# A hybrid decoder block's down projection as a 2x2 block product with seven block products

## What is computed

```
D_MODEL = 1024
D_FF = ((8 * D_MODEL + 3 * 256 - 1) // (3 * 256)) * 256        # 2816

def swiglu(hn, w_gate, w_up, w_down):
    return (jax.nn.silu(hn @ w_gate) * (hn @ w_up)) @ w_down

h = h + swiglu(rms_norm(h, norm_ffn_g[l]), w_gate[l], w_up[l], w_down[l])
return rms_norm(h, norm_final_g)
```

## Time and profile before

| | |
|---|---|
| median of three runs | 3043.88 us |
| the profiled execution's own time | 3043.22 us |
| its span, first to last instruction | 3041.5 us |
| PE (matmuls) busy | 2956.7 us, 97% |
| DVE busy | 1627.4 us, 54% |
| POOL busy | 1255.0 us, 41% |
| ACT busy | 1069.0 us, 35% |
| DMA: moved, mean rate | 297.39 MB, 98 GB/s |
| matmuls of both down projections | 2112 |
| mean granted clock of TensorE | 0.996 |

### The profile page before, as it was taken

The page is one execution under the profiler, slowest core; times in us unless marked ns, Lnnn a source line. Parts: engine busy times, 40 slices in busy tenths (PEclk is TensorE's granted clock), DMA queues, the critical chain, the costliest instruction groups (busy, mean ns, idle before and its releaser), DMA issues. The chain is left out here.

```text
span 3041.5 us, 41966 instructions
## 1 busy us (share of the span) xinstructions
PE 2956.7 (97%) x14334; PEld 2449.6 (81%) x14334; DVE 1627.4 (54%) x2236; ACT 1069.0 (35%) x1975; POOL 1255.0 (41%) x1126
## 2 busy tenths in 40 slices
PE   7999999999999999999999999999999999999998
PEld 7888788878878888878888778887888788887887
DVE  2564566645366444445565456665635644444445
ACT  4522445424233333322233244542423333332212
POOL 6422454452224444454442244445221444445433
PEclk9999999999999999999999999999999999999999
DMA  6622222141112222253322232224111122225221
GB/s 231 213 94 103 91 83 70 59 169 42 61 65 77 83 83 83 83 193 112 124 98 87 103 102 72 69 66 163 56 56 70 56 83 83 83 83 193 83 111 76
DMA packets 131685, 297.39 MB, mean 98 GB/s; under 512 B 11825, under 2 KB 52849, under 8 KB 131569
## 3 DMA queue, kind: packets, MB, share of 16 engines
q1 hardware_dynamic: 69072, 226.07, 21.4%
q10 hardware_dynamic: 62496, 69.78, 6.7%
HBM read 222.37 MB, written 73.43 MB: 97 GB/s over the span
## 5 line engine op out<-in xcount | busy, mean ns | idle before, releaser
L2409 DVE TENSOR_TENSOR h<-h,PS 128x1024 f32<-128x1024 f32 x272 | 330.9, 1220 | 332.0 <-PE PS L2588 214.9
L2586 PE MATMUL PS<-act_hi,w_hi 128*128 128x512 f32 (+1 forms) x1088 | 428.5, 394 | 9.5 <-issue 5.5
L1535 DVE TENSOR_TENSOR copied<-copied,PS 128x512 f32<-128x512 f32 x308 | 207.5, 685 | 400.9 <-PE PS L2588 387.9
L2588 PE MATMUL PS<-act_hi,w_lo 128*128 128x512 f32 (+1 forms) x1088 | 406.6, 374 | 0.0
L2587 PE MATMUL PS<-act_lo,w_hi 128*128 128x512 f32 (+1 forms) x1088 | 405.6, 373 | 0.0
L2050 POOL TENSOR_TENSOR w_lo<-raw,w_hi 128x256 fp32r<-128x256 f32 (+1 forms) x144 | 193.8, 1369 | 435.0 <-ACT w_hi L2127 435.0
L611 POOL TENSOR_TENSOR part_lo<-sum_s,part_hi 128x512 fp32r<-128x512 f32 x176 | 229.7, 1307 | 229.4 <-ACT part_hi L1060 229.4
L2586 PE MATMUL PS<-down,mid 128*128 128x512 f32 x704 | 276.6, 393 | 7.3 <-DVE h L2409 7.3
L2586 PE MATMUL PS<-op_t_hi,part_hi 128*128 128x512 f32 x704 | 275.3, 391 | 0.0
L2588 PE MATMUL PS<-down,mid 128*128 128x512 f32 x704 | 274.8, 390 | 0.0
L2587 PE MATMUL PS<-op_t_lo,part_hi 128*128 128x512 f32 x704 | 274.8, 390 | 0.0
(11 more groups left out here) (331 smaller groups left out, 6097.9 us busy)
## 6 DMA issues: line engine op xcount, KB each, us to landing
raw<-in_w_units SPq DMA_DIRECT2D x156, 512.0 KB, 3.9
gu_raw<-in_w_units SPq DMA_DIRECT2D x64, 512.0 KB, 5.1
a_d<-copied SPq DMA_DIRECT2D x88, 256.0 KB, 2.2
mid_raw<-a_d SPq DMA_DIRECT2D x44, 512.0 KB, 4.1
qkvz_d<-stage ACTq DMA_DIRECT2D x64, 256.0 KB, 2.7
raw<-att_d SPq DMA_DIRECT2D x32, 512.0 KB, 3.2
h<-in_x SPq DMA_DIRECT2D x12, 1024.0 KB, 7.9
prep_raw<-in_w_units SPq DMA_DIRECT2D x16, 512.0 KB, 4.4
```

Of the source, the lines that this page charges most:

```text
L1535: dve.tensor_tensor(buf[dst][:, :], buf[a][:, :], bank(k), ALU.add)\
L2409: dve.tensor_tensor(h[:, t, :], h[:, t, :], flat(bank(b + 2 * (t % 2), 2)), ALU.add)\
L2586: nc.tensor.matmul(out_ap, whi, xhi, start=start, stop=False)
L2588: return nc.tensor.matmul(out_ap, wlo, xhi, start=False, stop=stop)
```

## The change

The down projection of a half is now one product of 2x2 blocks: the activations A (1024 tokens x 2816) are halved in tokens, the weights B (2816 x 1024) in columns, and the inner dimension by the two rows of each pair. Seven block products with sums of blocks take the place of eight (`DOWN_OPS`). The sums of A's blocks are made in gate and up by DVE (`row_sums`, one after a pair's first row and three after its second) and stored beside A. The sums of B's blocks are made there too, in half 0 only (`column_sums`, four a pair) on rows which SP loads and stores for that (`load_t`, `store_t`, `t_d`).

The projection has 35 steps, five rounds of the seven products. In the first four rounds a step takes two parts (one of each of two pairs), in the last three. A part is a piece of weights and a piece of activations, 128x512 each, loaded into one of four raw buffers and split as one tile of 128x1024 by ACT and POOL, or for 7 parts of 77 by DVE (`vector_lo`). In a step PE makes four products of 128 tokens by 512 columns (24 or 36 matmuls) in six banks used in turn. DVE adds each to one or two of the sums `z6`, `h11`, `h12`, `h21` and `h22` (`down_add`); the h's are quarters of `h`. `z6` belongs to three of them and is added at steps 30 to 32 (`down_fold`). The next half's x tiles go with steps 8, 11, ... 29 (`X_STEPS`) and use banks 6 and 7. The final norm follows steps 33 and 34. A junk tile and the gate columns' banks in half 1 are moved too.

```diff
+DOWN_OPS = [("S2", "T2"), ("A11", "B11"), ("A12", "B21"), ("S4", "B22"), ("S1", "T1"), ("S3", "T3"),
+            ("A22", "T4")]
+DOWN_SUMS = [("z6",), ("z6", "h11"), ("h11",), ("h12",), ("h12", "h22"), ("h21", "h22"), ("h21",)]
+FOLDS = {30: ["z6 h12"], 31: ["z6 h21"], 32: ["z6 h22"]}
+DOWN_STEPS = 7 * (NPAIR // 2)
+DOWN_PARTS = 7 * NPAIR
+def on_vector(m):
+
+    return m % 6 == 2 and 14 <= m < FIRST_TRIPLE
...
+X_STEPS = {8 + 3 * i: i for i in range(TT)}
...
+            if m < 14:
+                k = (0, 0, 1, 1, 2, 2, 3, 3, 3, 5, 5, 6, 6, 5)[m]
+                act.wait_ge(S["prod_full"], prods(half, NPAIR - 1, 1, k))
+            else:
+                act.wait_ge(S["prod_full"], down_prods(half, step_of(m - 8)))
+            act.activation(flat(down_part[m][0][:, :, :]), flat(down_raw[m % 4][:, :, :]), ACT.Copy)\
+                .then_inc(S["copied" if on_vector(m) else "w_hi_ready"], 1)
...
+            dve.wait_ge(S["a_made"], of_f(half, j, s, 2, 2))
+            if s == 0:
+                total(1, one[3], one[0], one[2], ALU.subtract)
+            else:
+                total(2, two[3], one[2], two[2], ALU.add)
+                dve.wait_ge(S["a_stored0"], rows_stored(half, j + 1, 0))
+                total(3, one[3], two[2], one[3], ALU.subtract)
+                total(4, two[1], two[0], one[3], ALU.subtract)
...
+        def down_add(dve, half, s, p):
+
+            b = bank((4 * s + p) % 6)
+            dve.wait_ge(S["prod_full"], down_prods(half, s, p))
+            for name, (count, before) in zip(DOWN_SUMS[s % 7], ADDED[s, p]):
+                dst = partial(name, p)
...
+                if s == 0:
+                    dve.tensor_copy(dst, b).then_inc(S["joined"], 1)
+                else:
+                    dve.tensor_tensor(dst, dst, b, ALU.subtract if s % 7 == 6 else ALU.add)\
+                        .then_inc(S["joined"], 1)
+
+        def down_fold(dve, half, name, p):
+
+            src, dst = [partial(x, p) for x in name.split()]
+            dve.wait_ge(S["joined"], added(half, FOLDED[name, p][1]))
+            dve.tensor_tensor(dst, dst, src, ALU.add).then_inc(S["joined"], 1)
...
-                for q in range(1, DOWN_PASSES):
-                    down_hi(act, half, q)
...
+                for m in range(6, DOWN_PARTS):
+                    down_hi(act, half, m)
...
                 if half + 1 < NHALF:
-                    act.wait_ge(S["row_full1"], (half * ROW_PASSES + ROW_PASSES - 1) * 4)
+                    act.wait_ge(S["prod_full"], down_prods(half, step_of(71)))
                     for u in range(2):
                         split_hi(nth_load(half + 1, L_QKVZ, u), u, u)
...
+                for s in range(DOWN_STEPS):
+                    if s == DOWN_STEPS - 2:
+                        dve.wait_ge(S["gain_in"], gains(half, 3))
+                    for p in range(4):
+                        down_add(dve, half, s, p)
+                        if s >= DOWN_STEPS - 2 and p % 2 == 1:
+                            t = 2 * (s - DOWN_STEPS + 2) + p // 2
+                            norm_tile(h[:, t, :], h[:, t, :], gain, t % 2, norm_no(half, 3, t))
+                    for name in FOLDS.get(s, ()):
+                        for p in range(4):
+                            down_fold(dve, half, name, p)
...
+                for t in range(4, TT):
+                    norm_tile(h[:, t, :], h[:, t, :], gain, t % 2, norm_no(half, 3, t))
...
+            def down_step(half, s):
+
+                for m in parts_of(s):
+                    down_ready(pe, half, m)
+                for p in range(4):
+                    u = 4 * s + p
+                    if u < 6:
+                        pe.wait_ge(S["joined"], added(half, (3, 3, 3, 3, 4, 7)[u] - JOINS))
+                    else:
+                        pe.wait_ge(S["joined"], added(half, ADDED[(u - 6) // 4, (u - 6) % 4][-1][0]))
+                    ps = slice(p * P, (p + 1) * P)
+                    for m in parts_of(s):
+                        hi, lo = down_part[m]
+                        last = three(bank(u % 6), hi[:, 1, ps], lo[:, 1, ps], hi[:, 0, :], lo[:, 0, :],
+                                     m == parts_of(s)[0], m == parts_of(s)[-1])
+                    last.then_inc(S["prod_full"], 1)
```

More of the change, by code:

```diff
@@ L1878, in store_a @@
                 def store_a(j, s):
-                    made, row = of_f(half, j, s, 2, 2), bass.ds(j * 2 + s, 1)
+                    made = of_f(half, j, s, 2, 2)
+                    sums_done = s_count(half, j, 4 if s else 1)
+                    one, two = copied
                     sp.wait_ge(S["a_made"], made)
-                    for i, c in enumerate((0, 2)):
-                        sp.dma_start(a_d[row, :, i * CH:(i + 1) * CH]
-                                     .rearrange("n p c -> p (n c)"), copied[s][c][:, :])\
-                            .then_inc(S[f"a_stored{s}"], 16)
@@ L1886, in load_mid @@
[L1886 to L1895 removed]
+                    store_rows(j, s, [("A12", two[0]), ("A22", two[2])] if s else [("A11", one[0])])
@@ L1927, in _ @@
                         store_a(j, s)
+                        if half == 0:
+                            (store_t if s else load_t)(j)
                 last = NPAIR - 1
@@ L1930, in _ @@
                 sp.wait_ge(S["combined"], sums_made(half, last, 0, 4))
-                load_down(0)
-                load_h(1)
+                sp.wait_ge(S["raw_ready1"], gu_loads(half, last, 1))
+                sp.wait_ge(S["a_stored0"], rows_stored(half, last, 0))
+                sp.wait_ge(S["a_stored1"], rows_stored(half, last, 1))
+                sp.wait_ge(S["pr_stored1"], 64 + 32 * (NPAIR if half else last))
+                for m in range(2):
+                    load_part(m)
+                if half == 0:
+                    load_t(last)
@@ L1941, in _ @@
[L1941 to L1955 removed]
+                for m in range(4, 10):
+                    down_ready(sp, half, m - 4)
+                    load_part(m)
@@ new lines, in _ @@
+                store_a(last, 1)
+                if half == 0:
+                    store_t(last)
+                    sp.wait_ge(S["pr_stored1"], 64 + 32 * NPAIR)
+                sp.wait_ge(S["prod_full"], prods(half, last, 1, SPLITS - 1))
+                for k in range(2):
+                    load_h(k)
+                sp.wait_ge(S["a_stored0"], rows_stored(half, NPAIR, 0))
+                sp.wait_ge(S["a_stored1"], rows_stored(half, NPAIR, 1))
+                for k in range(2, 4):
+                    load_h(k)
```

383 lines of the change are left out of this document (233 added, 150 removed).

## The result

The changed kernel takes 3052.65 us (median of seven runs) against 3042.36 us for the kernel before on the same chip. The ratio is 1.0034 with a 95% interval of 1.0024 to 1.0044, so it is slower by a third of a per cent. A second series gave 1.003 (1.0017 to 1.0043). One of the seven runs took 6194 us, twice as long as the others, for a reason that is not on record; median and interval do not rest on it. The forecast was 3030 us, faster; the time lies in its range of 2998 to 3056, at the place of the first rival.

The account below looks back on a forecast made before the run. PE was taken to bound the kernel. Terms -59.8 - 4.6 (short waits behind x tiles) + 20 + 5 + 4 + 11 + 11 = -13.4 us on 3043.22 us gave 3030 us; 8-in-10 range 2998 to 3056 us.

Parts of the forecast that it names:

- Matmuls: Down projections: seven block products instead of eight, 924 matmuls a half instead of 1056, saving 59.8 us.
- Gate and up: Gate and up: DVE's added row and column sums fit in its slack, costing 0.
- Start: Start of both down projections: PE waits for DVE's sums and late h loads, plus lower clock; +20 us, bounds +2 and +28.
- Middle of half 0: Half 0's projection, middle steps: DVE sets the pace when its SBUF instructions wait for POOL; +5 us, bounds 0 and +19.
- Parts: Splitting and loading parts in the down projections: POOL keeps up with ten us in hand; cost 0.
- rival 1: Middle of half 0 and folds: DVE becomes the bound, always meeting POOL; middle costs 19 us, time 3053 us; chance 0.22.
- rival 2: DVE and POOL hardly meet at the ports; middle and folds cost 0, time 2998 us; sign: DVE idle mid-half 0; chance 0.15.
- Folds: Steps 30 to 32: z6 adds contend with POOL, PE waits in half 0, nearly all hidden in half 1; +4 us.
- End of half 0: Half 0's final norms delay ACT's ab_t copies, so PE stands 12 us; +11 us, bounds +6 and +16.
- End of half 1: After PE's last matmul: final norms, limited by two statistics slots, lengthen the tail; +11 us, bounds +5 and +22.
- rival 4: Gate and up no longer hides the sums: ten pairs of half 0 lose 3 us each; 3060 us; chance 0.07.
- rival 3: The clock: ten of PE's new waits each cost 1.3 us through a lower clock; 3043 us; chance 0.08.

Follow-up runs that it names:

- e5: e1 with both down projections' starts reordered: column sums earlier, row sums after step 1, loads of h and four parts before stores; 3005.3 us, ratio 0.9881.
- e1: The changed kernel with ACT's act_hi of an x tile one step earlier, ahead of two down_hi copies; 3029.6 us, ratio 0.9961 to the kernel before.
- e6: e1 with the final norms moved up and, in half 0, two weight-row splits between tiles 3 and 4; 3028.3 us, ratio 0.9953.
- e10: The changed kernel with DVE's own split of a part made one step earlier; 3035.5 us, ratio 0.9980 to the kernel before.

## Why the prediction was wrong

- **Matmuls, -59.8 us: right.** The account of e5's half 0 closes to a tenth of a us.
- **Gate and up, 0: right.** PE is busy for 100 of 100 us there, DVE for 69.
- **Start, +20 us: the mechanism right, a wait missed.** The waits of 9.3 and 6.4 us were measured as 9.2 and 6.4. The wait for `h` was 1.5 and 0.9 us in place of 4.6 and 1.9. But a part came late behind the loads of `h` and x (4.8 us, the POOL row of the waits), and the lower clock cost some 4 and 3 us where 2 and 2 were forecast. The first seven steps took 57.7 and 49.0 us for 38.1 us of matmuls: 19.6 and 10.9 us too long, where the forecast had 15.9 and 10.3.
- **Middle of half 0, +5 us: the step that failed.** The forecast summed DVE's durations over three steps and compared them with PE's. It never asked for what DVE waits in order. "Parts: 0, since POOL has ten us in hand" is the same fault: the slack was there, but DVE's split of every sixth part held SP's queue, and ACT's `act_hi` stood behind the loads. The middle cost 19 to 21 us in place of 5. That is the number of rival 1 (19) by a mechanism that is not rival 1's, so that the time came out at rival 1's 3053 is chance. The forecast's sign of rival 2, DVE idle in the middle of half 0, did appear, and meant the opposite of a fast kernel: DVE was idle because it stood in front of an instruction that was late.
- **Folds, +4 us: near in size, not in place.** DVE took 6.9, 7.5 and 2.5 us for its folds in half 0 and 6.9, 11.3 and 2.5 in half 1 (forecast 9.1, 6.8, 2.5). PE waited for 2.0 us in each half, where the forecast had 4 us in half 0 and nearly nothing in half 1; with the lower clock behind it this came to 2.3 and 3.9 us.
- **End of half 0, +11 us: right.** 11.8 us of waiting against 12.
- **End of half 1, +11 us: +7.** The pace of the tiles was as forecast (2.18 us a tile against 4.2 for two), but tile 3 (first row) was normalised by E+3.7, with E = 3035.2, and not at E+8.3:

```profile
3037.67 1.27 DVE L2590 SCALAR_TENSOR_TENSOR h<-h,stat_r,gain 128x1024 f32<-128x1024 f32 x1
3039.84 1.28 DVE L2590 SCALAR_TENSOR_TENSOR h<-h,stat_r,gain 128x1024 f32<-128x1024 f32 x1 [0.90 <-POOL stat_r L631]
...
3046.38 1.28 DVE L2590 SCALAR_TENSOR_TENSOR h<-h,stat_r,gain 128x1024 f32<-128x1024 f32 x1 [0.90 <-POOL stat_r L631]
```

- **Rivals.** PE's busy gate and up excludes rival 4. The clock (rival 3) had a part, but behind five waits and not ten: two at the start of half 0, one in its middle, one at the start and one at the end of half 1, at 1.8 to 2.7 us each. That is 10 us where the forecast had 4.
- **The sum.** The forecast was 22.7 us too low. In round numbers the middle makes 16 of them, the start 4, the stages ahead of the projection 4, the folds 2 and the end of half 0 1; the end of half 1 takes 4 back. e1, with the chain in the middle alone cut, runs in 3029.6 us. That this is the number forecast is in part luck: its middle costs almost nothing in place of 5 us and its tail 4 less, its start and folds 9 more.

## What to carry to other kernels

Adding up busy time per engine says whether a stage can be kept fed, not whether it will be. Where an instruction is added to an engine that runs in order, follow the buffer it frees to the queue that waits for it, and read what stands behind that wait; a loop that comes back to the same engine costs its full latency each round. And before moving work within an engine, see whether that engine has idle time at either place: if not, only shorter work helps.

## What the runs showed of the hardware

A DVE add of 128x512 with both operands in SBUF took 0.69 us alone and 2.8 us beside POOL's 128x1024 subtractions, also four times in a row (11.29 us). POOL's own took 2.35 to 2.4 us without such an add and 2.84 to 2.96 with one (e6, seven in 19.36 us). So in a steady row the two take turns, and the add, the shorter one, pays about four times what POOL's pays: some 2.1 us against 0.5. The column sums, of the same kind, ran at 0.69 us: POOL's splits had ended at 1352.1, half a us ahead of the first. The Trainium skill, "SBUF — State Buffer", section "Who interferes with whom", has the lock for whoever issues first. The trace agrees: the first add of a group that came ahead of POOL's split (2974.33 us in e6, the split at 2974.92) took 0.69 us.

The length of a wait alone does not tell whether the clock falls: at one and the same place 2.09 us (e5) passed without, 2.11 us (e10) did not. Nor does it at another: behind the same wait of 2.0 us in the last steps of half 0 the granted clock fell in e1 (0.61) and not in e5. Behind the waits at the start of the down projections that e5 took out, the clock had cost some 0.45 us for each us waited (5.5 for 12.8, 2.8 for 6.1). The forecast had 2 us for each start, whatever its length.
